# The last stage's tokens cut as 384 and 128 instead of twice 256, the final norm's weights applied on ScalarE, two wide products at the end, and the sums of two norms taken in two steps

## The reference, cut to what matters

```python
def rmsnorm_2(x, g):
    y = x * rsqrt(mean(x * x, axis=-1) + EPS)
    return y * g

h3 = rmsnorm_2(x, norm_ple_g)
ple = einsum('bse,ed->bsd', p, w_ple)                 # computed earlier, kept in DRAM
x = x + ple * sigmoid(einsum('bsd,de->bse', h3, w_ple_gate))
return rmsnorm_2(x, norm_final_g)
```

## Time and profile before

| | before |
|---|---|
| median of 3 runs | 2056.74 us (2056.51 to 2056.84) |
| the profiled execution's own time | 2056.55 us |
| its span | 2055.3 us |
| TensorE busy | 2021.4 us, 98% of the span |
| VectorE busy | 1089.9 us, 53% |
| ScalarE busy | 829.8 us, 40% |
| GpSimd busy | 292.9 us, 14% |
| granted TensorE clock, mean | 0.998 |

### The profile page before, as it was taken

One profiled execution on the slowest core, in us unless ns is written; L12 is line 12 of the kernel. 1 busy time (PEld: TensorE's weight loads), 2 busy tenths in 40 slices (PEclk: granted clock), 3 DMA queues, 4 the chain that ended last, 5 costly groups with the idle time before them and its releaser, 6 DMA issues.

```text
span 2055.3 us, 24093 instructions
## 1 busy us (share of the span) xinstructions
PE 2021.4 (98%) x9440; PEld 1686.0 (82%) x9440; DVE 1089.9 (53%) x1570; ACT 829.8 (40%) x1157; POOL 292.9 (14%) x219
## 2 busy tenths in 40 slices
PE   7999999999999999999999999999999999999998
PEld 5888888788888878888888888888788888888888
DVE  6665655624555654333336454544376575464666
ACT  5322223436665533222225455554434343242443
POOL 5000000001101200000000344443000021020130
PEclk9999999999999999999999999999999999999999
DMA  7755663422223523323222433333534332223232
GB/s 309 276 187 193 195 195 115 172 93 82 72 82 112 186 93 113 103 93 99 96 85 92 154 108 116 103 113 112 186 123 138 129 103 93 102 92 102 80 112 76
DMA packets 84401, 261.31 MB, mean 127 GB/s; under 512 B 9264, under 2 KB 13488, under 8 KB 84288
## 3 DMA queue, kind: packets, MB, share of 16 engines
q1 hardware_dynamic: 84288, 259.77, 37.5%
HBM read 242.92 MB, written 16.81 MB: 126 GB/s over the span
## 4 chain that ended last, share of the span: by engine, by line
PE 93%; DVE 3%; ACT 2%; issue 1%; DMA 0%; POOL 0%; SPq 0%; DVEq 0%; ACTq 0%; POOLq 0%
PE P L733 29%; PE P L734 29%; PE P L735 29%; PE P L935 1%; PE P L1101 1%; PE P L947 1%; PE P L946 1%; DVE SQ L1889 0%; ACT WH L588 0%; PE P L1148 0%; PE P L827 0%; DVE SL L2168 0%; DMA H<-x 0%; PE P L839 0%; ACT UH L1803 0%
## 5 line engine op out<-in xcount | busy, mean ns | idle before, releaser
L733 PE MATMUL P<-UH,WH 128*128 128x512 f32 (+1 forms) x1848 | 716.9, 388 | 5.9 <-POOL UL L2714 4.2
L734 PE MATMUL P<-UL,WH 128*128 128x512 f32 (+1 forms) x1848 | 713.4, 386 | 0.0
L735 PE MATMUL P<-UH,WL 128*128 128x512 f32 (+1 forms) x1848 | 713.3, 386 | 0.0
L588 ACT ACTIVATE WH<-WRAW 128x1024 fp32r<-128x1024 f32 (+1 forms) x345 | 359.1, 1044 | 813.3 <-PE P L735 809.6
L603 DVE TENSOR_TENSOR WL<-WRAW,WH 128x1024 fp32r<-128x1024 f32 (+1 forms) x286 | 356.0, 1248 | 205.2 <-ACT WH L588 204.5
L733 PEld LDWEIGHTS P<-UH,WH 128*128 128x128 f32 x1848 | 348.0, 188 | 75.3 <-issue 6.1
L735 PEld LDWEIGHTS P<-UH,WL 128*128 128x128 f32 x1848 | 347.6, 188 | 70.2
L734 PEld LDWEIGHTS P<-UL,WH 128*128 128x128 f32 x1848 | 347.8, 188 | 68.1
L733 PE MATMUL P<-AH,WH 128*128 128x512 f32 x544 | 212.1, 390 | 0.0
L734 PE MATMUL P<-AL,WH 128*128 128x512 f32 x544 | 211.7, 389 | 0.0
L735 PE MATMUL P<-AH,WL 128*128 128x512 f32 x544 | 211.7, 389 | 0.0
(11 more groups left out here) (273 smaller groups left out, 2235.8 us busy)
## 6 DMA issues: line engine op xcount, KB each, us to landing
WRAW<-w_gu SPq DMA_DIRECT2D x88, 512.0 KB, 3.5
ADA<-w_ada SPq DMA_DIRECT2D x72, 512.0 KB, 4.7
WRAW<-w_down SPq DMA_DIRECT2D x48, 512.0 KB, 3.5
WRAW<-w_up SPq DMA_DIRECT2D x44, 512.0 KB, 3.4
WRAW<-w_in SPq DMA_DIRECT2D x40, 512.0 KB, 3.5
WRAW<-w_mix SPq DMA_DIRECT2D x36, 512.0 KB, 3.5
WRAW<-w_down SPq DMA_DIRECT2D x24, 384.0 KB, 3.0
WRAW<-w_out SPq DMA_DIRECT2D x16, 512.0 KB, 4.1
```

Of the source, the lines that this page charges most:

```text
L588: s.act.activation(hi, s.mem.WRAW[:, c % 4, :self.order[c][2]], FN.Copy).then_inc(*self.rounded.inc(c))
L733: pe.matmul(out, wh, xh, start=start, stop=False, skip_group_check=True)
L734: pe.matmul(out, wh, xl, start=False, stop=False, skip_group_check=True)
L735: return pe.matmul(out, wl, xh, start=False, stop=stop, skip_group_check=True)
```

## The change

The last stage's two parts hold 384 and 128 tokens. ScalarE gets a new step, `gain`: it writes X times the final norm's weight into Y. `last` is then one VectorE product by the spread factor over several tiles: two tiles by 384 tokens in the first part, four tiles by 128 tokens in the second. The second part is stored with two DMAs of four tiles instead of four of two. `row` of the first part stands one product later, `last` of the first part stands later in VectorE's stream (its third call after the loop, its fourth behind the second part's `var`), and its stores are issued after all fetches of the embedding. Ahead of that, `pe_norm` takes the sums in two steps: one over the added squares of tiles 0 to 6, between the first two embedding products, and one over the square of tile 7, read from its own buffer, after the second; VectorE's addition of tile 7 goes away for these two norms.

```diff
+ENDS = [(0, 384), (384, 128)]
...
-        self.PLE = put("PLE", [128, 3, 256], F32)
+        self.PLE = put("PLE", [128, 3, ENDS[0][1]], F32)
...
+def pe_columns(s, src, b, at, n, first):
+
+    for tb in range(n):
+        last = s.pe.matmul(s.P[:, b, at + tb:at + tb + 1], src[:, tb * 128:(tb + 1) * 128],
+                           s.mem.ONE[:, 0:1], start=first and tb == 0, stop=True,
+                           skip_group_check=True)
+    return last
...
     pe_embedding(s, 4 * q, hi, lo)
+    s.on_pe.wait_ge(*s.small)
+    s.on_pe.wait_ge(*s.total(name, 0, KD - 2))
+    pe_columns(s, mem.SQ[:, 0, :], 7, 0, 4, True)
     pe_embedding(s, 4 * q + 1, hi, lo)
-    pe_sums(s, name, s.var(name), 0)
+    s.on_pe.wait_ge(*s.square(name, 0, KD - 1))
+    slot, _ = square_slot(s, name, 0, KD - 1)
+    pe_columns(s, mem.TMP[:, slot, :], 7, 0, 4, False).then_inc(*s.sums.inc(name, 0))
+    s.small = s.var(name)
...
-        hs = slice(256 * half, 256 * half + 256)
+        t0, n = ENDS[half]
+        hs = slice(t0, t0 + n)
...
-            last = mm3(pe, s.P[:, b, 0:256], (wh[:, cut], wl[:, cut]),
+            last = mm3(pe, s.P[:, b, 0:n], (wh[:, cut], wl[:, cut]),
...
-            for tb in range(2):
-                last = pe.matmul(s.P[:, 7, tb:tb + 1], src[:, tb * 128:(tb + 1) * 128],
-                                 mem.ONE[:, 0:1], start=n == 0 and tb == 0, stop=True,
-                                 skip_group_check=True)
+            last = pe_columns(s, src, 7, 0, ENDS[half][1] // 128, n == 0)
...
-        for tb in range(2):
+        for tb in range(ENDS[half][1] // 128):
...
-        if m == 3:
+        if m == 4:
             row(0)
...
-        act_ple(s, 4 * q + t, s.total(name, 0, 5 + t))
+        act_ple(s, 4 * q + t, s.total(name, 0, 5 + t) if t < 2 else s.sums(name, 0))
...
+    def gain(half, m):
+        act.activation(mem.Y[:, m, part(half)], mem.X[:, m, part(half)], FN.Copy,
+                       scale=s.col("norm_final_g", m)).then_inc(*s.xg.inc(half, m))
...
+        if n > 1:
+            gain(*divmod(n - 2, KD))
...
-    if m == 0:
+    if m == 0 or m == KD - 1 and name in ("ffn1", "mix"):
         return
...
-    def last(half, m0):
-        hs = slice(256 * half, 256 * half + 256)
-        for m in (m0, m0 + 1):
-            on.wait_ge(*s.row("end", half))
-            on.wait_ge(*s.x_end(half, m))
-            dve.scalar_tensor_tensor(mem.Y[:, m, hs], mem.X[:, m, hs], s.col("norm_final_g", m),
-                                     s.P[:, 6, 0:256], OP.mult, OP.mult).then_inc(
-                                         *s.o_row.inc(half, m))
+    def last(half, m0, tiles):
+        y, n = mem.Y[:, m0:m0 + tiles, part(half)], ENDS[half][1]
+        on.wait_ge(*s.row("end", half))
+        on.wait_ge(*s.xg(half, m0 + tiles - 1))
+        dve.tensor_tensor(y, y, s.P[:, 6, 0:n].unsqueeze(1).to_broadcast([128, tiles, n]),
+                          OP.mult).then_inc(*s.o_row.inc(half, m0))
...
-        if 12 <= n < 16:
-            last(0, 2 * n - 24)
+        if 14 <= n < 16:
+            last(0, 2 * n - 28, 2)
+    last(0, 4, 2)
     var(1)
-    for m in range(0, KD, 2):
-        last(1, m)
+    last(0, 6, 2)
+    last(1, 0, 4)
+    last(1, 4, 4)
...
     for n in range(2, 16):
         fetch(n)
-        if n >= 12:
-            store(0, 2 * n - 24)
     for m in range(0, KD, 2):
-        store(1, m)
-    on.wait_ge(*s.out_done(1, 6))
+        store(0, m, 2)
+    store(1, 0, 4)
+    store(1, 4, 4)
+    on.wait_ge(*s.out_done(1, 4))
```

More of the change, by code:

```diff
@@ L238, in __init__ @@
         self.ple_in = [new(f"ple_in{j}", [(n,) for n in range(j, 16, 3)], 16) for j in range(3)]
-        self.out_done = new("out_done", [(half, m) for half in range(2) for m in (0, 2, 4, 6)], 16)
+        self.out_done = new("out_done", [(0, 0), (0, 2), (0, 4), (0, 6), (1, 0), (1, 4)], 16)
         self.c_row = new("c_row", [()])
@@ L296, in __init__ @@
         self.sig = new("sig", [(half, m) for half in range(2) for m in tiles])
+        self.xg = new("xg", [(half, m) for half in range(2) for m in tiles])
         self.const_v = new("const_v", [("idb",), ("mask1",), ("mask2",), ("ntri",), ("none",)])
-        self.total = new("total", [e for e in squares if e[2]] +
+        self.total = new("total", [e for e in squares if e[2] and
+                                   (e[2] < KD - 1 or e[0] not in ("ffn1", "mix"))] +
                          [("end", half, m) for half in range(2) for m in range(1, KD - 1)])
@@ L356, in __init__ @@
         self.x_end = new("x_end", [(half, m) for half in range(2) for m in tiles])
-        self.o_row = new("o_row", [(half, m) for half in range(2) for m in tiles])
+        self.o_row = new("o_row", [(0, 0), (0, 2), (0, 4), (0, 6), (1, 0), (1, 4)])
         self.const_p = new("const_p", [("ones",), ("idf",), ("ntri",), ("m1",), ("m2",)])
@@ L825, in pe_sums @@
         s.on_pe.wait_ge(*s.total(name, acc, KD - 1))
[L826 to L831, removed]
-    s.small = var
+        pe_columns(s, s.mem.SQ[:, acc, :], b, 4 * acc, 4, acc == 0).then_inc(
+            *s.sums.inc(name, acc))
+    s.small = var
+def pe_columns(s, src, b, at, n, first):
[4 more added lines that the diff above has]
+    return last
 def pe_row(s, r, name, drained, b=6):
@@ L1206, in row @@
         on.wait_ge(*s.rstd("end", half))
-        for tb in range(2):
+        for tb in range(ENDS[half][1] // 128):
             last = pe.matmul(s.P[:, 6, tb * 128:(tb + 1) * 128],
                              mem.R[:, 4 * half + tb:4 * half + tb + 1].to_broadcast([128, 128]),
-                             mem.IDF[:, :], start=tb == 0, stop=tb == 1, skip_group_check=True)
+                             mem.IDF[:, :], start=tb == 0, stop=True, skip_group_check=True)
         last.then_inc(*s.row.inc("end", half))
-        s.drained[6] = [s.o_row(half, KD - 1)]
+        if half == 0:
+            s.drained[6] = [s.o_row(0, 6)]
     for m in range(KD):
@@ L1834, in act_last, with part @@
     act, on, mem, W = s.act, s.on_act, s.mem, s.W
+    def part(half):
+        t0, n = ENDS[half]
+        return slice(t0, t0 + n)
     def sigmoid(half, m):
-        x = mem.Y[:, m, 256 * half:256 * half + 256]
+        x = mem.Y[:, m, part(half)]
         on.wait_ge(*s.e_raw(half, m))
@@ L1843, in square @@
         if m == 0:
-            dst = mem.SQ[:, half, 0:256]
+            dst = mem.SQ[:, half, 0:ENDS[half][1]]
             on.wait_ge(*(s.score("b", 15) if half else s.sums("ffn3", 0)))
@@ L1847, in square @@
             slot, e = square_slot(s, "end", half, m)
-            dst = mem.TMP[:, slot, 0:256]
+            dst = mem.TMP[:, slot, 0:ENDS[half][1]]
             on.wait_ge(*e)
-        act.activation(dst, mem.X[:, m, 256 * half:256 * half + 256], FN.Square).then_inc(
+        act.activation(dst, mem.X[:, m, part(half)], FN.Square).then_inc(
             *s.square.inc("end", half, m))
+    def gain(half, m):
+        act.activation(mem.Y[:, m, part(half)], mem.X[:, m, part(half)], FN.Copy,
+                       scale=s.col("norm_final_g", m)).then_inc(*s.xg.inc(half, m))
     for n in range(18):
@@ L2617, in total @@
             on.wait_ge(*s.total("end", half, m - 1))
-        dve.tensor_tensor(mem.SQ[:, half, 0:256], mem.SQ[:, half, 0:256],
-                          mem.TMP[:, end_slot(half, m), 0:256], OP.add).then_inc(
+        n = ENDS[half][1]
+        dve.tensor_tensor(mem.SQ[:, half, 0:n], mem.SQ[:, half, 0:n],
+                          mem.TMP[:, end_slot(half, m), 0:n], OP.add).then_inc(
                               *s.total.inc("end", half, m))
     def add(half, m):
-        n, hs = half * KD + m, slice(256 * half, 256 * half + 256)
+        n, hs = half * KD + m, part(half)
         e, x = mem.Y[:, m, hs], mem.X[:, m, hs]
@@ L2626, in add @@
         on.wait_ge(*s.ple_in[n % 3](n))
-        dve.tensor_tensor(e, e, mem.PLE[:, n % 3, :], OP.mult).then_inc(*s.e_ple.inc(half, m))
+        dve.tensor_tensor(e, e, mem.PLE[:, n % 3, 0:ENDS[half][1]], OP.mult).then_inc(*s.e_ple.inc(half, m))
         on.wait_ge(*s.e_ple(half, m))
@@ L2632, in gate @@
     def gate(half, m):
-        hs = slice(256 * half, 256 * half + 256)
+        hs = part(half)
         on.wait_ge(*s.gate_mm(half, m))
@@ L2636, in gate @@
         on.wait_ge(*s.a_lo_p(NF - 1))
-        dve.tensor_tensor(mem.Y[:, m, hs], s.psum("ple gate", half, m)[:, 0:256],
+        dve.tensor_tensor(mem.Y[:, m, hs], s.psum("ple gate", half, m)[:, 0:ENDS[half][1]],
                           mem.RR[:, hs], OP.mult).then_inc(*s.e_raw.inc(half, m))
@@ L2642, in var @@
         on.wait_ge(*(s.rstd("end", 0) if half else s.rstd("ffn3")))
[L2643 removed]
+        n = ENDS[half][1] // 128
+        dve.tensor_scalar(mem.VAR[:, 0:n], s.P[:, 7, 0:n], 1.0 / D, EPS, OP.mult,
                           OP.add).then_inc(*s.var.inc("end", half))
[L2646 to L2653 removed]
+    def last(half, m0, tiles):
[4 more added lines that the diff above has]
```

(13 more changed lines are left out.)

## The result

| | before | changed |
|---|---|---|
| median | 2056.62 us (4 runs) | 2074.63 us (4 runs, 2074.16 to 2074.99) |
| span of the profiled execution | 2055.3 us | 2073.0 us |
| granted TensorE clock, mean | 0.998 | 0.988 |

What follows compares the result with a forecast made beforehand. Bound by TensorE's matmul stream up to 2044 us, then a tail going through one engine at a time. Terms +8.6 - 0.8 + 0.5 - 3.2 + 1.6 = +6.7 us on 2056.74 gave 2063.4 us, 0.33% slower, range 2060.0 to 2067.0.

Steps and rivals of the forecast that it cites:

- the clock: Rival, second part of the last stage: TensorE's clock falls, some 20 us more at half clock, 2083 us; chance 0.03.
- Products, +8.6 us: Last stage's matmul stream: 384-token matmuls at 0.173 us and 128-token ones at 0.112 us, 54.7 us against 46.1 us.
- 8.6 - 0.8 + 0.5: Last stage: products +8.6 us, waits absorbed by longer products -0.8 us, more records for first part's sums and row +0.5 us.
- The wait in the first product: Stage's first product: TensorE's 0.63 us wait for the input's low part is no longer seen; within the -0.8 us.
- the gap ahead of the sums: Behind the stage's first product: sums start at 1997.48 where 1997.15 would do; covered too, within the -0.8 us.
- The page's 81 ns: Rival, second part: 81 ns per 128-column matmul, 6.0 us less, so +0.7 us in all, 2057.4 us; chance 0.04.
- The other engines: Stream: ScalarE and VectorE don't starve TensorE; rival that they fall behind, 2 to 4 us more, chance 0.07.
- The tail, -3.2 us: From the last product to the span's end: shorter instructions, sums, power, row and last VectorE products, -3.2 us (-4.2 to -2.2).
- the 0.2 us for `last` ahead of the variance: Tail: VectorE runs a first-part `last` of 0.95 us ahead of `var(1)`, while square and sums take about 0.75: +0.2 us.
- The norms, +1.6 us: Two norms: four more float32 columns between the first two embedding products, +0.8 us each, +1.6 us (0 to +2.0).
- 128-token products at the pace of their columns: Rival, second part: 0.067 us a matmul, 12.9 us for the part, sum -1.9 us, 2054.8 us; chance 0.06.

Runs made afterwards that it cites:

- all three profiled falls: The changed kernel, 2074.63 us; the same kernel run again unchanged, 2074.71 us; and the change with its parts swapped, 128 tokens first, 2088.27 us.
- The two widened kernels: The changed kernel with all three, or only one in three, of the second part's matmuls streaming 256 tokens: 2064.91 us (ratio 1.0032) and 2063.08 us (1.0027).

## Why the prediction was wrong

Its direction holds and so do most of its steps; its size doesn't, for one step: the clock, a term that the sum put at nothing. I read the granted clock of the 128-token stretch at 1521.8 us as evidence, said that it "lasted only 1.70 us", and still gave the fall a chance of 0.03 and no place in the range. The stage would have 21 us of such matmuls. The runs show the fall in each profiled execution of a kernel with that part unwidened, at 6 to 12 us into it. My price for it, 20 us for the whole part, was sound too: 105 matmuls at 0.213 instead of 0.112 us are 10.7 us, and the first part's row at half the clock, 1.24 us from 2047.97 to 2049.21, adds some 0.7. Together that is 11.4 us, and the forecast was 11.2 us too low. That the two come so close is in part luck, as terms below were off in both directions.

Term by term:

- *Products, +8.6 us.* The 384-token ones stand 0.173 us apart and the 128-token ones 0.112 us at the full clock, both as forecast. With the 11.4 us of the clock taken off, the stage is 8.3 us longer, which is what my terms 8.6 - 0.8 + 0.5 give. The wait in the first product and the gap ahead of the sums are gone, as expected.
- *The page's 81 ns* (the Trainium skill, "TensorE: Matmul & The Clock Gate", section "Back-to-back issue gap") is not what this part shows: its first three products, 72 matmuls at the full clock, take from 2029.87 to 2037.86, where the sums start: 8.0 us, 0.11 us each. The measurement decides.
- *The other engines.* None starved TensorE; it is busy in all of the stage. With the widths undone, ScalarE's extra 5.5 us left the stage at 50.3 us.
- *The tail, -3.2 us.* It was -3.1 us, with pieces that were off both ways. The row took 0.81 us instead of 0.64, the sums 0.60 instead of 0.35, the power 0.55 instead of 0.45. I had `last` of the first part's tiles 6 and 7 run beside the chain; it is on it, since the row is written to bank 6 and must wait until that `last` has read the bank: it ended at 2068.18, the power at 2067.94. Against that, the 0.2 us for `last` ahead of the variance didn't appear, and the last store landed 2.7 us after VectorE's end instead of 3.0.
- *The norms, +1.6 us.* Mis-sized: about +0.9 us. From the end of the first of the four embedding products to the start of the last it takes 5.57 us instead of 5.55 at the first norm and 6.48 instead of 5.56 at the second. The columns cost 0.9 us at each (0.8 themselves, and a slower start of the matmul behind them), and at the first the power gave it back, a coupling between VectorE and GpSimd that I hadn't looked for, though its rows (1.92 us against 0.71 for half the columns) stood in my table. The other 0.3 us of the stage's later start was there before the first norm, in the execution with the lower clock in its first 40 us.

The rival that ended on the other side, 128-token products at the pace of their columns, was out by the first stretch. The rival of the clock came true.

## What to carry to other kernels

Before cutting a stream of matmuls into narrower pieces, price each piece by the start-to-start distance of that width in the trace: here 128 tokens cost 0.112 us and 256 cost 0.120. And ask how long the narrow ones run in a row, since with them TensorE can be busy all the time and still lose its clock; a short stretch of them elsewhere in the trace at full clock is no evidence. Where a small instruction of GpSimd stands on the chain, look at what VectorE starts just ahead of it.

## What the runs showed of the hardware that I had not expected

- A TensorE that waits for nothing is brought to 1.2 GHz within a run of matmuls of 128 columns, and comes back to 2.4 GHz among matmuls of 384 columns, 2.9 us after the first of them. The Trainium skill, "TensorE: Matmul & The Clock Gate", section "Why this matters for your kernels", asks for TensorE to be kept busy without idle gaps. The trace here has no gap and the clock falls, so that is not enough. What amount of columns would have been enough isn't settled by these runs.
- In all three profiled falls the one-column matmuls of a norm's sums, 0.9 to 1.3 us of them, had ended 1.5 to 2.5 us before (at 2039.16 for the fall at 2040.8 in the changed kernel). The two widened kernels have the same sums between the same products and kept the clock, so the sums alone don't bring it down; narrow matmuls without them weren't tried.
- The same narrow matmuls with more columns that nobody reads are faster as a whole: 2063.1 and 2064.9 us against 2074.6 (ratios 1.0027 and 1.0032 against 1.0082).
- GpSimd's power over four columns takes 1.01 us, and 1.92 us when a VectorE instruction of 1.22 us has started 0.16 us ahead of it: it ends 0.9 us after that one's end. When the power starts first, by 0.15 us, VectorE's instruction keeps its 1.23 us. The runs show the times; that it is the shared ports is the page's account, named with the experiment, and it fits only the first of these two orders.
